# Four seven-product units in most gate-and-up pairs, the first one's sums on GpSimd, and thirteen such units in each down projection

## The reference, cut to what matters

```
def swiglu(h, w_gate, w_up, w_down):
    return (jax.nn.silu(h @ w_gate) * (h @ w_up)) @ w_down

for i in range(DEPTH):                      # DEPTH = 2
    ...
    x = x + jnp.concatenate([tok, cross], axis=-1) @ w_out
    x = x + swiglu(rms_norm(x, norm_ffn_g[i]), ffn_w_gate[i], ffn_w_up[i], ffn_w_down[i])
```

## Time and profile before

| | |
|---|---|
| median of 3 runs | 2365.40 us (2365.35 to 2365.51) |
| the profiled execution, its own time | 2365.48 us |
| its span, first to last instruction | 2363.7 us |
| PE busy | 2357.4 us, 100% of the span |
| DVE busy | 1738.3 us, 74% |
| ACT busy | 1228.2 us, 52% |
| POOL busy | 53.8 us, 2% |
| mean DMA rate | 187 GB/s |

### The profile page before, as it was taken

One profiled execution on the slowest core, in us unless ns is written; L12 is line 12 of the kernel. 1 busy time (PEld: TensorE's weight loads), 2 busy tenths in 40 slices (PEclk: granted clock), 3 DMA queues, 4 the chain that ended last, 5 costly groups with the idle time before them and its releaser, 6 DMA issues.

```text
span 2363.7 us, 29178 instructions
## 1 busy us (share of the span) xinstructions
PE 2357.4 (100%) x10610; PEld 1910.4 (81%) x10610; DVE 1738.3 (74%) x2145; ACT 1228.2 (52%) x1529; POOL 53.8 (2%) x60
## 2 busy tenths in 40 slices
PE   9999999999999999999999999999999999999999
PEld 7888888888888888888888888888888888888887
DVE  6555666656989988858787546655989988758876
ACT  6645555545655645545454454444655655545443
POOL 1000110000000000000000000000000000000000
PEclk9999999999999999999999999999999999999999
DMA  7665555445655656555555755555565655555564
GB/s 253 196 195 158 163 161 161 152 168 178 196 196 177 204 186 201 190 188 187 196 189 194 233 159 169 174 178 182 179 206 181 199 195 190 193 188 193 194 210 151
DMA packets 230690, 441.13 MB, mean 187 GB/s; under 512 B 14637, under 2 KB 18866, under 8 KB 230322
## 3 DMA queue, kind: packets, MB, share of 16 engines
q1 hardware_dynamic: 224274, 430.01, 55.7%
q10 hardware_dynamic: 6304, 9.61, 1.2%
HBM read 437.45 MB, written 2.12 MB: 186 GB/s over the span
## 4 chain that ended last, share of the span: by engine, by line
PE 98%; DVE 1%; ACT 0%; DMA 0%; issue 0%; POOL 0%; ACTq 0%; POOLq 0%; DVEq 0%
PE bank L587 26%; PE bank L586 26%; PE bank L585 26%; PE bank L680 5%; PE bank L682 5%; PE bank L681 5%; PE bank L607 2%; PE bank L802 1%; PE bank L827 0%; DVE w_lo L1388 0%; PE bank L656 0%; PE bank L776 0%; PE bank L751 0%; PE bank L814 0%; DMA raw<-in_mem_w_kv_dram 0%; DVE aT_lo L1517 0%
## 5 line engine op out<-in xcount | busy, mean ns | idle before, releaser
L1388 DVE TENSOR_TENSOR w_lo<-raw,w_hi 128x1024 fp32r<-128x1024 f32 (+1 forms) x816 | 945.5, 1173 | 534.8 <-ACT w_hi L976 533.7
L976 ACT ACTIVATE w_hi<-raw 128x1024 fp32r<-128x1024 f32 (+1 forms) x816 | 827.8, 1019 | 830.1 <-PE bank L587 782.9
L587 PE MATMUL bank<-w_hi,hT_lo 128*128 128x512 f32 x1680 | 669.6, 399 | 0.0
L585 PE MATMUL bank<-w_hi,hT_hi 128*128 128x512 f32 x1680 | 668.9, 398 | 0.0
L586 PE MATMUL bank<-w_lo,hT_hi 128*128 128x512 f32 x1680 | 662.2, 394 | 0.0
L587 PE MATMUL bank<-w_hi,aT_lo 128*128 128x512 f32 x976 | 388.9, 398 | 0.0
L585 PE MATMUL bank<-w_hi,aT_hi 128*128 128x512 f32 x976 | 387.1, 397 | 0.6 <-DVE w_lo L1388 0.6
L586 PE MATMUL bank<-w_lo,aT_hi 128*128 128x512 f32 x976 | 385.1, 395 | 0.0
L586 PEld LDWEIGHTS bank<-w_lo,hT_hi 128*128 128x128 f32 x1680 | 315.8, 188 | 77.0
L587 PEld LDWEIGHTS bank<-w_hi,hT_lo 128*128 128x128 f32 x1680 | 315.5, 188 | 73.7
L585 PEld LDWEIGHTS bank<-w_hi,hT_hi 128*128 128x128 f32 x1680 | 315.6, 188 | 72.9
(11 more groups left out here) (179 smaller groups left out, 1983.1 us busy)
## 6 DMA issues: line engine op xcount, KB each, us to landing
raw<-in_ffn_w_gate_dram SPq DMA_DIRECT2D x176, 512.0 KB, 3.6
raw<-in_ffn_w_up_dram SPq DMA_DIRECT2D x176, 512.0 KB, 4.5
raw<-in_ffn_w_down_dram SPq DMA_DIRECT2D x176, 512.0 KB, 4.4
raw<-in_a_w_in_dram SPq DMA_DIRECT2D x104, 512.0 KB, 3.5
raw<-in_b_w_in_dram SPq DMA_DIRECT2D x72, 512.0 KB, 3.6
raw<-in_a_w_out_dram SPq DMA_DIRECT2D x40, 512.0 KB, 3.5
raw<-in_b_w_out_dram SPq DMA_DIRECT2D x40, 512.0 KB, 4.2
raw<-in_mem_w_kv_dram SPq DMA_DIRECT2D x32, 512.0 KB, 4.6
```

Of the source, the lines that this page charges most:

```text
L585: nc.tensor.matmul(o, hi[:, k, rows], w_hi[:, slot, a, :], start=(first and a == 0), stop=False)
L587: last = nc.tensor.matmul(o, lo[:, k, rows], w_hi[:, slot, a, :], start=False, stop=(last_one and a == CHUNK_KT - 1))
L976: nc.scalar.activation(w_hi[:, slot, 0:tiles], raw[:, slot, 0:tiles], ACT.Copy).then_inc(hi_ready, 1)
L1388: nc.vector.tensor_tensor(w_lo[:, slot, 0:tiles], raw[:, slot, 0:tiles], w_hi[:, slot, 0:tiles].bitcast(F32), ALU.subtract).then_inc(chunk ...
```

## The change

In the gate-and-up plans:

- GATE_UP (pairs 1 to 7 of each layer) has four units of seven products, (2, 3, 5, 6), where it had three, (2, 4, 6). The two that it had in GATE_UP_FIRST and in GATE_UP_LATE remain two, at other places.
- In pairs 1 to 9, POOL makes the three subtractions of the pair's first such unit (its own `sum_weights`, called by `sum_pair`); DVE waits there for `weights_summed`, ahead of its low split of the unit's first chunk. DVE makes those of the other units, as before.
- Where both fall on one chunk, `low_sums` of the earlier unit now stands ahead of `sum_weights` of the next one.
- One more set of mixes is made per layer, since four units need them; units 2 and 3 are both made at the stream's second quarter.

In the down projection DOWN[0] has 7 such units (before 6) and DOWN[1] 6 (before 5), and there are two buffers for the sums of the weights in place of one.

In all there are 47 units of seven products in each layer (2 + 7 x 4 + 2 x 2 + 7 + 6) where there were 38 (2 + 7 x 3 + 2 x 2 + 6 + 5). The diff, without the lines that place buffers and pass them on:

```
-GATE_UP, GATE_UP_FIRST = Plan(IN_CHUNKS, (2, 4, 6)), Plan(IN_CHUNKS, (4, 6))
-GATE_UP_LATE, GATE_UP_LAST = Plan(IN_CHUNKS, (2, 6)), Plan(IN_CHUNKS)
+GATE_UP, GATE_UP_FIRST = Plan(IN_CHUNKS, (2, 3, 5, 6)), Plan(IN_CHUNKS, (5, 6))
+GATE_UP_LATE, GATE_UP_LAST = Plan(IN_CHUNKS, (2, 5)), Plan(IN_CHUNKS)
...
-DOWN = (Plan(DOWN_CHUNKS, (4, 7, 10, 13, 16, 19)), Plan(DOWN_CHUNKS, (5, 8, 11, 14, 17), TAIL_UNITS))
+DOWN = (Plan(DOWN_CHUNKS, (4, 6, 9, 11, 14, 16, 19)), Plan(DOWN_CHUNKS, (5, 7, 10, 12, 15, 17), TAIL_UNITS))
...
-            if pair == 0:
-                return [gate_up_sums[1], gate_up_sums[0]]
-            return [gate_up_sums[(pair + i) % 2] for i in range(len(GATE_UP.sevens))]
+            return [gate_up_sums[i % 2] for i in range(len(plan_of(pair).sevens))]
...
                     ahead = c + AHEAD
-                    if ahead in plan.first:
-                        sum_weights(weights[plan.first.index(ahead)])
                     if ahead in plan.after:
                         low_sums(weights[plan.after.index(ahead)])
+                    if ahead in plan.first:
+                        i = plan.first.index(ahead)
+                        if i == 0 and 0 < pair < PAIRS:
+                            dve.wait_ge(weights_summed, tally.at("seven", 1))
+                            last_buffer[0] = weights[i]
+                        else:
+                            sum_weights(weights[i])
...
         @block.gpsimd
         def _(pool):
...
+            def sum_weights(weights, used):
+                ring_turn, slot = ring_place(tally)
+                b11, b21, b12, b22 = range(CHUNK_KT * slot, CHUNK_KT * slot + 4)
+                total = weights[2]
+                for s in (slot, slot + 1):
+                    pool.wait_ge(raw_loaded[s], ring_turn * 16 + 16)
+                wait(pool, sums_used, used)
+                link(nc.gpsimd.tensor_tensor(total[:, 0:2, :], raw_tiles[:, b22:b21:-1, :], raw_tiles[:, b21:b22 + 1:2, :],
+                                             ALU.subtract))
+                link(nc.gpsimd.tensor_tensor(total[:, 2, :], raw_tiles[:, b12, :], total[:, 0, :], ALU.subtract))
+                nc.gpsimd.tensor_tensor(total[:, 3, :], raw_tiles[:, b11, :], total[:, 2, :], ALU.subtract
+                                        ).then_inc(weights_summed, 1)
...
+                if norm in (N_FFN0, N_FFN1):
...
+                    with pool.Fori(0, (LATE - 2) // TURN_PAIRS) as turn:
+                        tally.enter(turn)
+                        for pair in (1, 2):
+                            sum_pair(pair)
+                        tally.leave((LATE - 2) // TURN_PAIRS)
+                    for pair in range(LATE - 1, PAIRS - 1):
+                        sum_pair(pair)
```

More of the change, by code:

```diff
@@ L276, in trunk @@
         mv = sb("mv", [P, TOK, 2])
-        guest.enter_context(nc.sbuf_tensor("kept_h", [P, KT + KT // 2, SEQ], F32))
-        down_raw = guest.enter_context(nc.sbuf_tensor("down_raw", [P, 4, BLOCK], F32))
+        guest.enter_context(nc.sbuf_tensor("kept_h", [P, KT, SEQ], F32))
+        down_raw = [guest.enter_context(nc.sbuf_tensor(f"down_raw{i}", [P, 4, BLOCK], F32)) for i in range(2)]
         guest.close()
@@ L314, in trunk @@
         tenant.close()
+        used_raw = tsb("used_raw", [P, 4, BLOCK])
+        tenant.close()
         tsb("kept_e", [P, FT - 4 * HPB, SEQ])
@@ L416, in per_turn @@
             return dict(chunk=PAIR_CHUNKS * pairs, t=pairs, y=pairs, split_t=2 * pairs, evac=pairs, sq=0, sums=0, pow=0,
-                        step=(2 * len(GATE_UP.sevens) + 3) * pairs, seven=len(GATE_UP.sevens) * pairs, partial=pairs,
+                        step=(2 * len(GATE_UP.sevens) + 1) * pairs, seven=len(GATE_UP.sevens) * pairs, partial=pairs,
                         gate=TOK * pairs, mix=0)
@@ L959, in _ @@
                     events = {DOWN_NEXT: [("final", 1)]}
-                run_pair(PAIRS + 1, DOWN[1], hidden_T, down_sums, banks, events, fresh=True, end=(layer == 1))
+                run_pair(PAIRS + 1, DOWN[1], hidden_T, down_sums[1], banks, events, fresh=True, end=(layer == 1))
                 parity[0] ^= 1
@@ L1363, in _ @@
                     events = {2: [lambda: store(0), lambda: store(1)], DOWN_DONE_T: [lambda: store(2)]}
-                run_pair(PAIRS + 1, DOWN[1], down_sums, banks, events, mixes[1], end=(layer == 1))
+                run_pair(PAIRS + 1, DOWN[1], down_sums[1], banks, events, mixes[1], end=(layer == 1))
                 parity[0] ^= 1
@@ L1518, in low_part @@
                                                                   high[:, a, :], ALU.mult, ALU.subtract)
-                if place is None:
+                if units:
+                    mix_tiles(units, gain_row)
+                else:
                     last.then_inc(T_free, 1)
-                else:
-                    mix_tiles(place, gain_row)
                 tally.add("t")
@@ L1611, in stage2 @@
                     row = STREAM_GAIN[j // QT]
-                    place = MIX_PLACE[2 * (j % QT)] if j // QT in (0, 2) and j % QT in GATE_UP_PARTS else None
-                    low_part(hT_lo[:, part, :], hT_hi[:, part, :], lambda a: row + (j % QT) * HPB + a, place)
+                    units = [u for u in GATE_UP.sevens if u // 2 == j % QT] if j // QT in (0, 2) else []
+                    low_part(hT_lo[:, part, :], hT_hi[:, part, :], lambda a: row + (j % QT) * HPB + a, units)
                     if j % QT == QT - 1:
@@ L1911, in _ @@
                 events[0] = [take_last]
-                run_pair(PAIRS, DOWN[0], down_sums, banks, events, mixes[0], half=0)
+                run_pair(PAIRS, DOWN[0], down_sums[0], banks, events, mixes[0], half=0)
                 first_adds = pair_banks(PAIRS, *banks)[0]
@@ L1931, in _ @@
                                    DOWN_DONE_T: [lambda: stage2("stream", QT + 2)]})
-                run_pair(PAIRS + 1, DOWN[1], down_sums, banks, events, mixes[1], half=1, end=(layer == 1))
+                run_pair(PAIRS + 1, DOWN[1], down_sums[1], banks, events, mixes[1], half=1, end=(layer == 1))
                 parity[0] ^= 1
@@ L1946, in _, with sum_pair @@
         def _(pool):
-            steps = [0]
+            tally = Tally(dict(step=2 * TURN_PAIRS, chunk=PAIR_CHUNKS * TURN_PAIRS, seven=len(GATE_UP.sevens) * TURN_PAIRS))
             def link(ins):
                 ins.then_inc(pool_step, 1)
-                steps[0] += 1
-                pool.wait_ge(pool_step, steps[0])
+                tally.add("step")
+                pool.wait_ge(pool_step, tally.at("step"))
+            def sum_weights(weights, used):
[10 more added lines that the diff above has]
+                                        ).then_inc(weights_summed, 1)
+            def sum_pair(pair):
+                start = tally.n["chunk"]
+                tally.n["chunk"] = start + plan_of(pair).first[0]
+                sum_weights(buffers(pair)[0], tally.at("seven", 0 if buffers(pair)[0] is buffers(pair - 1)[-1] else -1))
+                tally.n["chunk"] = start + PAIR_CHUNKS
+                tally.add("seven", len(plan_of(pair).sevens))
             nc.gpsimd.memset(halves[:, :], -0.5)
@@ L1968, in _ @@
                                         ).then_inc(pow_given, 1)
+                if norm in (N_FFN0, N_FFN1):
+                    layer = (N_FFN0, N_FFN1).index(norm)
+                    blocks = 4 + sum(len(b) for b in (A_BLOCKS, B_BLOCKS)[:layer + 1])
+                    tally.n["chunk"] = (IN_CHUNKS * blocks + QT * OUT_CHUNKS * (layer + 1) + PAIR_CHUNKS
+                                        + layer * (PAIRS * PAIR_CHUNKS + QT * DOWN_CHUNKS))
+                    per_layer = sum(len(plan_of(p).sevens) for p in range(PAIRS)) + sum(len(p.sevens) for p in DOWN)
+                    tally.n["seven"] = layer * per_layer + len(GATE_UP_FIRST.sevens)
+                    with pool.Fori(0, (LATE - 2) // TURN_PAIRS) as turn:
[5 more added lines that the diff above has]
+                        sum_pair(pair)
 _INS = ["x", "mem", "rel_bias", "norm_mix_g", "norm_mem_g", "norm_ffn_g", "mem_w_kv", "mem_q_norm_g",
```

57 lines of the change are left out of this document (35 added, 22 removed).

## The result

The changed kernel takes **2386.1 us** (median of 4 runs, 2385.97 to 2386.87) where the kernel before takes 2365.4 (4 runs beside them, 2365.35 to 2365.51): 1.0087 times the time, 95% interval 1.0075 to 1.0099. It is 20.7 us slower. The forecast was 2379.

The account below looks back on a forecast made before the run. PE (matmuls) was taken to bound the kernel, with DVE nearest to making it wait. 14 loop pairs growing from 43.56 to 44.7 give +16.0, down halves -2.8: 2365.5 + 13.2 = 2379 us; 8-in-10 range 2353 to 2400.

Parts of the forecast that it names:

- 54 matmuls, 12.6 us; down halves -2.8: 18 more units, each 3 matmuls less: 9.8 us in loop pairs, 2.8 in down halves, counted there in full without stall.
- POOL and DVE exclude each other instruction by instruction: While either reads two SBUF tensors, or POOL any, the other engine is held; DVE then goes on at 8.0, not 6.4.
- POOL's sums at 4.4 us: POOL's three subtractions for a pair's first unit: 1.89 + 1.03 + 1.03 us plus waits; lower bound 2.2, upper 6.2.
- The 2387: Kernel time if POOL's subtractions cost the skill's 4497 ns for 2048 columns, putting POOL's end 0.6 us later.
- The product held once, DVE on at +8.0: Loop pair: product of gate and up waits to 5.60, ends 6.93; POOL's third follows to 7.96, then DVE goes on.
- Unit 2's low sums at 9.98: Loop pair: DVE's low sums of unit 2 come at 9.98 us, ACT's part of them taking until then.
- The chain behind it: After unit 2's low sums: chunk 11 loads at 18.0, lands 22.5; unit 6 subtractions 29.3, low sums 33.95 to 36.25.
- PE stands 1.8 in all, period 44.7: Loop pair: 42.86 us of PE work plus 1.8 of waiting, 1.1 more than now; 14 pairs give +16.0 us.
- Where PE waits: Loop pair: PE idle before chunk 6 and before the last 12 matmuls of units 3 and 6, released by DVE.
- The free port: Faster rival: POOL and DVE do not hold each other off; DVE on at 6.4, period 43.0, 2355 us; chance 0.32.
- Only POOL is held: No-change rival: only POOL is held, or it gets in between; period 43.5 to 44.1, 2362 to 2370; chance 0.13.
- Slower still: Rival: POOL's subtractions take 6.2 us (2405), or loads in quick succession land later than 4.5 us; chance 0.13.

Follow-up runs that it names:

- The fifth experiment: Changed kernel with DVE making the hidden tile's low part ahead of unit 3's three subtractions, not behind them; 2386.6 us, ratio 1.0088.

## Why the prediction was right, and by how much it was off

The direction and the mechanism were right: the result is 7 us above the forecast, inside its case (2371 to 2390). Part of the closeness is luck, as said below.

- **54 matmuls, 12.6 us; down halves -2.8.** Right: 119.20 and 119.00 us with PE unbroken, and 2362.7 for the down halves alone.
- **POOL and DVE exclude each other instruction by instruction.** Right, and shown from both sides: held splits and products in the changed kernel, none when POOL reads no tensors. The Trainium skill's rule (SBUF — State Buffer, "Who interferes with whom") agrees for subtractions on both engines. For the power the trace differs from the page's "whole instruction", as the earlier trace rows had it already: a split that starts 0.6 into a power is not held (749.35 and 749.95 above).
- **POOL's sums at 4.4 us.** Too low: 5.0 unheld, 5.2 with the gaps that the 4.4 had in it. The first ended at +4.79, not 4.33, and the second at +6.16, not 5.60. The Trainium skill's price (GPSIMD Engine Reference, "Elementwise — side-by-side cycle accounting") would be 4.5 for the 2048 columns as one instruction; the measured three come to 5.0. The 2387 that the forecast worked out from that price is within 1 us of the result, but by chance: it had DVE go on 0.6 later than 8.0, and DVE went on 0.33 later.
- **The product held once, DVE on at +8.0.** The order was wrong in a small way. The forecast held the whole product to 6.93 and let POOL's third run behind it; in fact that one falls between the two halves and ends at 7.86, and the second half ends behind it. DVE goes on at 8.33. Here two errors cancel in part: the forecast's order with the measured sizes would give 6.16 + 1.33 + 1.30, about 8.8 (an estimate). Nor was it foreseen that POOL begins ahead of the split in 5 of 14 pairs, where DVE goes on at 8.11 to 8.66.
- **Unit 2's low sums at 9.98.** Measured 10.07. This is the step from which all later ones hang, and the 0.3 by which DVE was later was nearly absorbed by the wait for ACT that was already in the forecast.
- **The chain behind it.** Chunk 11's load at 18.0 (17.97), landed 22.5 (22.38), unit 6's subtractions at 29.3 (29.33), its low sums at 33.95 (33.98), in the pair shown.
- **PE stands 1.8 in all, period 44.7: the mis-sized term.** The mean is 45.14, and 14 x 0.44 = 6.2 us, nearly the whole error. About 0.26 of it is in every pair: with the landing at 22.5 I put the period at 44.7, while the measured line gives 22.5 + 22.46 = 44.96. From the landing to unit 6's low sums it is 11.6 us and not 11.45, and a restart of PE costs 0.1 us beyond its wait: the second matmul comes 0.33 behind the first (858.72 and 859.05 in the pair shown) in place of 0.233. The rest, 0.17, is that the landing's mean over the 14 pairs is 22.67, one load at 23.87 among them.
- **Where PE waits.** Two appointments were left out: the transposes, which wait for the product (up to 0.84 us in a pair, 0.3 in the mean), and unit 2's third product, which waits for the hidden tile's low part (0.25 to 0.5). Unit 3's low sums then cost 0.34 and not 0.95. The fifth experiment shows that this moves the cost and does not add to it.
- **Pairs 8 and 9.** The wait for POOL was to cost nothing there. It cost 0.17 us in pair 8 of each layer and nothing in pair 9.
- **The rivals.** The free port (2355) would have been right if POOL did not read: half the pairs of that experiment ran at its period. "Only POOL is held" (2362 to 2370) fails by the held product and the held splits. "Slower still" was not met; loads were late by its amount in one pair only.

What stays open: why chunk 11's load takes 5.1 to 6.3 us in the first loop pair of layer 0, in every variant with unit 3, where it takes 4.4 to 4.8 in the others. That was not tried.
